# A four-layer hybrid decoder on one core: each tile's trip through DRAM is read back in the slot of its writes

## The reference

```python
def reference(x, ...):
    for i in range(DEPTH):                       # 4
        hn = rmsnorm(x, norm_g[i])
        if kind == 0:   y = diff_attention(hn, da_w_in[j], da_w_out[j], ...)
        elif kind == 1: y = sliding_window_attention(hn, sw_w_in[j], sw_w_out[j], ...)
        else:           y = mlstm(hn, ml_w_in[j], ml_b_gates[j], ml_w_out[j], ...)
        x = x + y
    return rmsnorm(x, final_g)
```

## Time and profile before

| | |
|---|---|
| runs | 1713.46 us median of 3, 1713.16 to 1715.52 |
| profiled execution, own time | 1715.07 us |
| its span, first to last instruction | 1713.3 us |
| TensorE busy | 1701.4 us, 99% of the span |
| VectorE, ScalarE, GpSimd busy | 1189.6, 911.0, 38.4 us |
| moved by DMA | 364.53 MB, 213 GB/s mean |
| granted TensorE clock, mean | 0.999 |

### The profile page before, as it was taken

The page is one execution under the profiler, slowest core; times in us unless marked ns, Lnnn a source line. Parts: engine busy times, 40 slices in busy tenths (PEclk is TensorE's granted clock), DMA queues, the critical chain, the costliest instruction groups (busy, mean ns, idle before and its releaser), DMA issues.

```text
span 1713.3 us, 24445 instructions
## 1 busy us (share of the span) xinstructions
PE 1701.4 (99%) x7890; PEld 1419.4 (83%) x7890; DVE 1189.6 (69%) x1909; ACT 911.0 (53%) x1400; POOL 38.4 (2%) x99
## 2 busy tenths in 40 slices
PE   9999999999999999999999999999999999999998
PEld 7888888888878888888888888888888888888887
DVE  7768676775759888865656465656666686777756
ACT  7454555454556666755555445454554555455543
POOL 1000000000000000000000000000000000000000
PEclk9999999999999999999999999999999999999999
DMA  8768677766875555478999699966877686767663
GB/s 284 241 190 261 208 238 218 231 215 220 263 210 160 163 156 157 149 234 198 189 166 269 178 201 185 262 182 218 253 233 239 193 266 198 248 215 232 225 233 127
DMA packets 230035, 364.53 MB, mean 213 GB/s; under 512 B 14950, under 2 KB 80044, under 8 KB 229836
## 3 DMA queue, kind: packets, MB, share of 16 engines
q1 hardware_dynamic: 229536, 362.94, 73.2%
q10 hardware_dynamic: 380, 0.56, 0.1%
q0 software_dynamic: 48, 0.13, 0.1%
HBM read 335.79 MB, written 27.79 MB: 212 GB/s over the span
## 4 chain that ended last, share of the span: by engine, by line
PE 94%; DMA 3%; DVE 1%; issue 1%; SPq 1%; ACT 0%; DVEq 0%; POOLq 0%; POOL 0%; ACTq 0%
PE acc L1136 29%; PE acc L1138 28%; PE acc L1137 28%; PE tp L1102 1%; PE tp L1136 1%; PE tp L1137 1%; PE tp L1138 1%; PE sc L1137 1%; PE sc L1136 1%; PE sc L1138 1%; SPq L566 0%; DMA shared<-k_turning 0%; DMA qs<-q_turning 0%; PE sc L1162 0%; DMA th<-x_turning 0%
## 5 line engine op out<-in xcount | busy, mean ns | idle before, releaser
L2015 DVE TENSOR_TENSOR w_lo<-raw,w_hi 128x1024 fp32r<-128x1024 f32 x583 | 703.4, 1220 | 399.7 <-ACT w_hi L1074 397.1
L1074 ACT ACTIVATE w_hi<-raw 128x1024 fp32r<-128x1024 f32 x583 | 609.8, 1056 | 452.7 <-PE acc L1138 401.2
L1136 PE MATMUL acc<-w_hi,xt_hi 128*128 128x512 f32 x1824 | 715.6, 392 | 2.6 <-DVE xt_lo L1499 1.4
L1138 PE MATMUL acc<-w_hi,xt_lo 128*128 128x512 f32 x1824 | 711.1, 390 | 0.0
L1137 PE MATMUL acc<-w_lo,xt_hi 128*128 128x512 f32 x1824 | 710.7, 390 | 0.0
L1138 PEld LDWEIGHTS acc<-w_hi,xt_lo 128*128 128x128 f32 x1824 | 342.5, 188 | 72.4
L1136 PEld LDWEIGHTS acc<-w_hi,xt_hi 128*128 128x128 f32 x1824 | 342.8, 188 | 70.8 <-DVE w_lo L2015 1.9
L1137 PEld LDWEIGHTS acc<-w_lo,xt_hi 128*128 128x128 f32 x1824 | 342.8, 188 | 67.8
L1136 PE MATMUL acc<-w_hi,ot_hi 128*128 128x512 f32 (+1 forms) x456 | 176.6, 387 | 0.0
L1138 PE MATMUL acc<-w_hi,ot_lo 128*128 128x512 f32 (+1 forms) x456 | 175.8, 386 | 0.0
L1137 PE MATMUL acc<-w_lo,ot_hi 128*128 128x512 f32 (+1 forms) x456 | 175.8, 385 | 0.0
(11 more groups left out here) (306 smaller groups left out, 1229.5 us busy)
## 6 DMA issues: line engine op xcount, KB each, us to landing
raw<-in_da_w_in_dram SPq DMA_DIRECT2D x255, 512.0 KB, 4.3
raw<-in_ml_w_in_dram SPq DMA_DIRECT2D x96, 512.0 KB, 5.6
raw<-in_sw_w_in_dram SPq DMA_DIRECT2D x72, 512.0 KB, 3.7
raw<-in_da_w_out_dram SPq DMA_DIRECT2D x64, 512.0 KB, 4.0
raw<-in_sw_w_out_dram SPq DMA_DIRECT2D x32, 512.0 KB, 3.6
raw<-in_ml_w_in_dram SPq DMA_DIRECT2D x64, 256.0 KB, 7.9
raw<-in_ml_w_out_dram SPq DMA_DIRECT2D x32, 512.0 KB, 4.3
qs<-q_turning SPq DMA_DIRECT2D x12, 512.0 KB, 7.0
```

What stands on the lines that cost most here:

```text
L1074: act.activation(w_hi[:, q:q + 2, :], raw[:, 2 * p:2 * p + 2, :], ACT.Copy).then_inc(hi_ready, 1)
L1136: pe.matmul(out_ap, k_hi, m_hi, start=start, stop=False)
L1138: return pe.matmul(out_ap, k_lo, m_hi, start=False, stop=stop)
L2015: dve.tensor_tensor(w_lo[:, two, :], raw[:, two, :], w_hi[:, q:q + 2, :].bitcast(F32), ALU.subtract).then_inc(lo_ready, 1)
```

## The change

In four tables the slot of every read becomes the slot of its writes. Before, a read stood two slots behind its writes. Now SyncE issues the four writes, waits until they have landed, issues the read, and only then goes on to the weight load of the next slot. Nothing else is touched.

```diff
-           read=(24, 26, 33, 41), split=(24, 26, 33, 40), gain=(20, 22, 29), total=(37,))
+           read=(22, 24, 31, 39), split=(24, 26, 33, 40), gain=(20, 22, 29), total=(37,))
...
-DA = dict(q_evac=11, q_turn=12, q_write=19, q_read=21, q_copy=20, k_evac=19, k_turn=20, k_write=27, k_read=29, k_copy=28,
+DA = dict(q_evac=11, q_turn=12, q_write=19, q_read=19, q_copy=20, k_evac=19, k_turn=20, k_write=27, k_read=27, k_copy=28,
```

More of the change, by code:

```diff
@@ L59 @@
 TWO = dict(order=out_order((0, 1), (2, 3)), end=(14, 16, 24, 32), sum=(18, 20, 27, 35), write=(22, 24, 31, 39),
-           read=(24, 26, 33, 41), split=(24, 26, 33, 40), gain=(20, 22, 29), total=(37,))
+           read=(22, 24, 31, 39), split=(24, 26, 33, 40), gain=(20, 22, 29), total=(37,))
 THREE = dict(order=out_order((0, 1, 2), (3,)), end=(20, 22, 24, 32), sum=(24, 26, 28, 35), write=(29, 31, 33, 39),
-             read=(31, 33, 35, 41), split=(30, 32, 34, 40), gain=(26, 28, 30), total=(37,))
+             read=(29, 31, 33, 39), split=(30, 32, 34, 40), gain=(26, 28, 30), total=(37,))
 OUT = {"da": THREE, "sw": dict(TWO, split=(24, 26, 33, 37), turn=(33,)), "ml": TWO}
 MOVED = {"da": 4, "sw": 3, "ml": 4}
-DA = dict(q_evac=11, q_turn=12, q_write=19, q_read=21, q_copy=20, k_evac=19, k_turn=20, k_write=27, k_read=29, k_copy=28,
-          v_evac=27, score=25, softmax=29, diff=(31, 33), p_turn=34, p_write=39, p_read=41, p_copy=40, pv=(37, 38), ssq=(41, 42),
-          g_tanh=35, gate=36, mix=45, o_write=50, o_read=52, o_split=54, o_split_last=51)
+DA = dict(q_evac=11, q_turn=12, q_write=19, q_read=19, q_copy=20, k_evac=19, k_turn=20, k_write=27, k_read=27, k_copy=28,
+          v_evac=27, score=25, softmax=29, diff=(31, 33), p_turn=34, p_write=39, p_read=39, p_copy=40, pv=(37, 38), ssq=(41, 42),
+          g_tanh=35, gate=36, mix=45, o_write=50, o_read=50, o_split=54, o_split_last=51)
 SW = dict(kv_evac=3, sink_set=10, v_stage=14, k_T=5, k_hi=9, k_lo=(10, 13), q_evac=11, q_T=11, q_hi=(15, 16), q_lo=(15, 15, 17, 18),
@@ L73 @@
           o_gate=(26, 28), o_hi=(27, 29), o_lo=(29, 30))
-ML = dict(qk_evac=11, q_turn=12, q_write=17, q_read=19, qk_copy=19, score=(17, 18), decay=(18, 19), weigh=(21, 22),
+ML = dict(qk_evac=11, q_turn=12, q_write=17, q_read=17, qk_copy=19, score=(17, 18), decay=(18, 19), weigh=(21, 22),
           v_evac=19, pv=(20, 21), den=25, ssq=26, comb=29, o_tanh=27,
-          g_tanh=35, gate=36, mix=37, o_write=43, o_read=45, o_split=45)
+          g_tanh=35, gate=36, mix=37, o_write=43, o_read=43, o_split=45)
 COUNTS = {
```

## The result

| | before | after |
|---|---|---|
| median of the runs, us | 1713.31 | 1721.84 |
| their range, us | 1712.2 to 1715.52 (4 runs) | 1720.58 to 1724.12 (4 runs) |
| span of the profiled execution, us | 1713.3 | 1722.4 |
| mean granted clock in it | 0.999 | 0.997 |

A forecast was written before the change was run, and what follows sets the result against it. The prediction took TensorE, busy 1701.4 of 1713.3 us, as the bound. Its terms, +4.4 - 0.9 - 0.3 = +3.2 us, gave 1718.3 for the profiled execution and 1716.7 us as a median, range 1712.0 to 1722.0.

The forecast's parts named there:

- rival 2: Diff-attention, six crossings of o and q: o's read may take 6.3 us, q lands late, 4.5 us slower, 1721.2; chance 0.20.
- What bounds the kernel; little to gain: Whole run: TensorE is busy nearly throughout and waits 3.0 us, so earlier transfers can give back at most 0.18%.
- mLSTM, third round, +4.4: Third mLSTM round: holds at o's and q's reads dry the full queue twice, 2 x 2.2 us, reaching TensorE: +4.4 us.
- A gap of 2.2: Price of each pause in SyncE's queue while writes land, in an otherwise full stretch: 2.2 us.
- Layer boundary, -0.9: Layer boundary: the last quarter of x is read ahead of two loads, shortening TensorE's 1.4 us wait for xt_lo: -0.9 us.
- the third quarter's read, two tiles earlier, gets later by about 1.4: Layer boundary: three tiles queue one behind the other with landings between, delaying this read 1.4 us and leaving 1.1 of 2.5.
- Crossing of o and q, 0: Diff-attention, six times: o's read goes out earlier, q comes no later, held loads have 0.9 us of cover: 0 us.
- First k read, -0.3: First k read: it loses the load ahead of it, so TensorE's 0.3 us wait at its score goes: -0.3 us.
- k, p and the other moves, 0: Moves of p, the other k and the first q: a lead of eight slots, 21.8 us, hides some 4 us: 0.
- Rival 1: Full stretch: engines keep moving older loads, the gap vanishes and only gains remain, -1.2 us, 1712.3; chance 0.19.
- rival 3: All 51 reads: every one pays a gap of 2.2 us, 112 us together, 1826; chance 0.01.

The follow-up runs named there:

- the median of that part: Only the reads of o and q in diff-attention moved (16 of the 51), against the kernel before: 1714.95 us, ratio 1.0011.
- the mLSTM part: Only the reads of o and q in mLSTM moved (8 of the 51), against the kernel before: 1718.59 us, ratio 1.0033.
- the x part: Only the reads of the residual stream's quarters moved, at all boundaries (11 of the 51), against the kernel before: 1714.62 us, ratio 1.0011.

## Why the prediction was right or wrong

The sign came out right, and for the reason given: held loads in a stretch without slack. The size did not: of the 8.5 us the sum had 3.2. That 1721.84 lies inside the range is for the most part luck: the range reaches up to 1722.0 for rival 2 alone, its six crossings at 4.5 us, and of the rest came only 2.5 us from three crossings; the clock and the boundary made the remainder.

- *What bounds the kernel; little to gain:* right. No variant gained more than about 1 us by the medians.
- *mLSTM, third round, +4.4:* right in place and chain. The size was met too, in one profile by luck: +4.4 in the changed kernel, but 1.7 of it is clock, and +4.4 in that part alone, without any fall of the clock. The first two rounds, counted at nothing, added 0.4 and 1.0 in these profiles. A gap of 2.2 was met by 1.8 and 2.2 of share, 1.5 and 1.6 by the rate. (The 294 GB/s behind the price were read in the last 2 us of the full stretch, not behind it.) That the wait shows as q_lo was foreseen in part: the held load's split does stand ahead of the copies of k and q.
- *Layer boundary, -0.9:* **this is the step that failed**, in its sub-step "the third quarter's read, two tiles earlier, gets later by about 1.4". It landed 4.2 us later, and +2.7 us net came of the step in the profile (1.7 of it clock). The 1.4 stood there without a working; what I had not counted were two holds in a row, of 4.6 and 4.3 us, in which neither writes nor loads of the next tile go out; the second quarter's writes took 8.5 us from the first issue to the landing (447.31 to 455.80), before 6.3. The other half of the step, a read that lands sooner when it stands ahead of its loads, held: 3.3 us in place of 6.3.
- *Crossing of o and q, 0:* mis-sized. At the place that I had worked through it came out as forecast: from the first write of o to q's landing 15.0 us now (forecast 15.1, before 16.0), and no wait followed. But at the first crossing of the last layer it took 17.0 (before 16.5), and there a wait decided that I had not named. VectorE may rotate k (its position embedding) only when q's writes have left the tile in which both work:

```profile
1398.91 0.69 DVE L1560 TENSOR_TENSOR shared<-shared,cos_a 128x512 f32<-128x512 f32 x1 [3.88 <-DMA q_turning<-shared]
...
1406.15 1.18 DVE L2015 TENSOR_TENSOR w_lo<-raw,w_hi 128x1024 fp32r<-128x1024 f32 x1
```

  Its subtraction came at 1406.15, behind k's rotation, q's split and k's transposition, and TensorE waited 1.1 us, until 1407.38. This chain is read from the trace; no run tests it, and in two kernels that leave the place alone TensorE waits 0.3 us there too. Rival 2 had the place, not the size (+1.8 by the median of that part, 4.5 forecast), and a wrong mechanism: the read of o took 3.4 us there, not 6.3; it was q's writes that took 6.5 from the first issue to the landing.
- *First k read, -0.3:* the wait went, but that can't be put down to the change. It is absent also from the profiles of the mLSTM part and of the x part, in which k is as before. The wait for xt_lo varies in the same way: 1.4 us in the kernel before, 0.2 in the kernel with only mLSTM's o moved. A single short wait in one profile is no sure gain.
- *The clock:* missing from the sum, 3.4 us in the profile. The rows of before show 9 tenths or more all along, and 1.00 in the earlier trace rows; I took that for a property of the kernel.
- *k, p and the other moves, 0:* right for k and p by their own run, for the rest by the profile alone. *Rival 1* (the gap is filled) and *rival 3* (each wait costs) are out. The Trainium skill's rule to wait late ("DMA: Bandwidth & Descriptors", section "Rules for kernel authors") matters here at a handful of places; the others can break it for nothing; the trace agrees with it where weights have no slack.

## What to carry to other kernels

Where weights arrive just in time, the queue that issues them should not stand on a semaphore while it has loads to give: one load ahead of the waiting instruction took away about three quarters of the loss here. Price a hold by the stage, by what the stage's DMA share and the next wait for its loads leave, and where tiles follow each other count every hold in the chain, with the writes that it keeps back. And where TensorE starts to wait, allow for its clock: a fall cost 1.7 us here, and it did not come behind every wait.

## What was not expected of the hardware

The clock does not follow the length of one wait. In the changed kernel TensorE was busy 2.10 of the 4 us ahead of 478, and the clock fell to its lower level; with only mLSTM's o moved it was busy 1.73 of 4 us, idle for longer, and the clock stayed up. The changed kernel, then the other:

```profile
474.00:478.00 4.00, 2.10 (x10) 1.43 (x9) 2.79 (x3) 3.97 (x8) 0.00 (x0) 1.00 0.88 271
```

```profile
1029.00:1033.00 4.00, 1.73 (x10) 1.55 (x11) 2.04 (x6) 2.04 (x5) 0.00 (x0) 1.00 0.99 171
```

What decides between the two stays open. The two falls in the changed kernel cost 1.7 us each, about as much as the waits ahead of them; so a wait of 2 us can cost nearly 4.
